# Prompt attention in rounds of four units: scores and weighings of four in a row, the turns in pairs around them, outputs copied by four

## The chip, the cores and the metric

The kernel runs on one core of a Trainium2 chip. The metric is the device time of one execution in microseconds, the median of several runs. All times below are microseconds unless marked ns. Engines: PE is TensorE, DVE is VectorE, ACT is ScalarE, POOL is GpSimd, SP is the engine whose queue issues most transfers.

## What is computed

One layer of a decoder trunk over 2048 prompt tokens and 32 sample tokens: a joint input projection, attention and a convolution module side by side, an output projection, and an MLP. The change touches only the prompt attention. There are 8 heads of 64 and three patterns (window, dilation); the queries of a head are cut into 16 blocks of 128, and each block sees its own 128 keys and, except at the start of a residue class, the 128 before them.

```python
DILATED_PATTERNS = ((128, 1), (512, 4), (2048, 16))
...
logits = jnp.einsum('brnqhd,brnkhd->brnhqk', qb, kc, ...) * (HEAD_DIM ** -0.5) + bias
logits = jnp.where(valid[None, None, :, None], logits, -jnp.inf)
m = jnp.max(logits, axis=-1)
e = jnp.exp(logits - m[..., None])
l = jnp.sum(e, axis=-1)
acc = jnp.einsum('brnhqk,brnkhd->brnqhd', e, vc.astype(jnp.float32))
```

m, l and acc of the three patterns are merged in a later stage.

## The kernel before

The kernel is written with one instruction stream for each engine and semaphores between them; nothing reorders the streams. Its stages run one after the other, with a barrier of all engines between them. The prompt attention is the stage whose tiles are named `pa_`.

Its work is a list of 192 units `(hp, p, t)`: head pair `hp` (4), pattern `p` (0, 1, 2), block of queries `t` (16), in this order. A unit does both heads of its pair. Whether it has a previous block of keys is `has_prev`: in pattern 0 all units but the first, in pattern 1 three of four (not `t` = 0, 4, 8, 12), in pattern 2 none. A unit with one works on 256 keys a head, a unit without on 128. A unit u goes through:

- scores(u), PE: 2 matmuls (one a head, on 64 rows of the array each) into `s_ps`. The trace shows each of these float32 matmuls as two records. Two units share a bank per head, and there are two such banks per head, so unit u waits until unit u-3 has left.
- lower(u), DVE: 2 instructions add the bias, take the extreme and write `score`, four units deep.
- exponential(u), ACT: 2 instructions, in place in `score`.
- turn(u), PE: one transpose for each head and block of keys, 4 (or 2) of 128x128, into `t_ps`, which is two units deep.
- copy_turned(u), DVE: one copy from `t_ps` into `probT`, which is three units deep: it waits for `o_pe`, the count of units weighed, to reach u-2, that is until unit u-3 has been weighed.
- weigh(u), PE: 4 (or 2) matmuls of the values with `probT` into `oT_ps`, on 64 columns of the array each; here too each is two records.
- the result goes from `oT_ps` to `oT` by a copy on ACT, is transposed back by PE (back) into `o_ps`, and copied by DVE into `o_sb`, from where it is stored.

PE, DVE and ACT each run a loop over steps of two units. PE's step s holds the scores of units 2s and 2s+1, the turns of 2s-2 and 2s-1, the back of step s-4 and the weighings of 2s-4 and 2s-3. `oT_ps`, `oT` and `o_ps` hold two units. ACT does in each step the copy of `oT_ps`, four exponentials and, for four of every eight units where the target half is of pattern 1 or 2, a query piece (`query_piece`: a 128x256 copy into `query_run`, from which the scores of the unit eight places later read; 16 pieces a head pair). POOL regroups keys (`key_runs`) and works off part of the convolution.

Of the kernel before, what the change touches and what calls it, by code (L numbers as in the profile page):

```python
# [15 lines left out]
P = 128  # L16
# [78 lines left out]
def build(nc, I, O):  # L95
# [22 lines left out]
    with whole:  # L118
# [104 lines left out]
        with conv:  # L223
# [1172 lines left out]
            with ExitStack() as st:  # L1396
# [30 lines left out]
                oT = sb("oT", [P, 2, 2, P])  # L1427
# [6 lines left out]
                oT_ps, o_ps = ps("oT_ps", [P, 2, P]), ps("o_ps", [P, 2, P])  # L1434
# [13 lines left out]
                STEPS = N // 2  # L1448
# [60 lines left out]
                with nc.Block() as block:  # L1509
                    @block.sync  # L1510
                    def _(sp):
# [29 lines left out]
                        for q in range(3 * PAIRS):  # L1541
                            hp, p = divmod(q, 3)
                            for half in range(2):
# [12 lines left out]
                                sp.wait_ge(o_done, (q * NT + (half + 1) * NT // 2) // 2)  # L1556
# [48 lines left out]
                    def _(pe):  # L1605
# [25 lines left out]
                        def weigh(u):  # L1631
# [5 lines left out]
                            if u >= 2 and u % 2 == 0:  # L1637
                                pe.wait_ge(oT_done, u // 2)
                            for j in range(1 + prev):
                                for hh in range(2):  # L1640
                                    part = slice(hh * DH, hh * DH + DH)
                                    mm = pe.matmul(oT_ps[part, u % 2], vp[hp % 2][:, p, t - prev + j, part],
# [3 lines left out]
                        def back(s):  # L1646
                            pe.wait_ge(oT_done, s + 1)
                            if s >= 1:
                                pe.wait_ge(o_done, s)
                            for i in range(2):  # L1650
                                mm = pe.transpose(o_ps[:, i], oT[:, s % 2, i], ident[:])
                            mm.then_inc(back_pe, 1)

                        for s in range(STEPS + 4):
                            if s < STEPS:
                                scores(2 * s)
                                scores(2 * s + 1)
                            if 1 <= s < STEPS + 1:
                                turn(2 * s - 2)
                                turn(2 * s - 1)  # L1660
                            if s >= 4:
                                back(s - 4)
                            if 2 <= s < STEPS + 2:
                                weigh(2 * s - 4)
                                weigh(2 * s - 3)

                    @block.vector
                    def _(v):
# [25 lines left out]
                        def out_pair(s):  # L1694

                            ch, i = divmod(s, NT // 4)
                            v.wait_ge(back_pe, s + 1)
                            if i == 0 and ch >= 2:
                                v.wait_ge(o_out[ch % 2], out_count(ch - 2))
                            v.tensor_copy(o_sb[:, ch % 2, 2 * i:2 * i + 2], o_ps[:]).then_inc(o_done, 1)  # L1700
# [1602 lines left out]
```

## Time and profile before

| | us |
|---|---|
| median of 3 runs (2705.34 to 2710.91) | 2708.74 |
| profiled execution, own time | 2703.57 |
| its span, first to last instruction | 2701.8 |
| prompt attention, first scores to last output copy | about 614.0 to 886.4 |
| in that stage, one head pair | about 67 |

Read it so: the durations below come from the one profiled execution, whose own time stands 5.17 under the median. The stage is a tenth of the span and has a barrier at its end, so what it takes longer or shorter moves everything behind it.

### The profile page before, as it was taken

To read this page: it belongs to the slowest core of one execution; us is meant where nothing else is said; L and a number is where in the kernel's file an instruction comes from. 1 tells how busy PE (TensorE), PEld (TensorE's weight loads), DVE (VectorE), ACT (ScalarE), POOL (GpSimd) and SP (SyncE) were. 2 spreads that over 40 slices of the span, in tenths; PEclk is the share of its full clock that TensorE was granted. 3 is DMA by queue.
4 is the path that set the end of the run, shared out by engine and by line. 5 is a ranking of instruction groups with operands and counts; after the bars stand their busy time and mean duration, and the time that the engine had idled before them with its cause. 6 is when DMAs were issued, how large, how long until landed. Compare 5 with 4: busy or idle time off the path is not lost.

```text
span 2701.8 us, 45845 instructions
## 1 busy us (share of the span) xinstructions
PE 2571.1 (95%) x16346; PEld 2278.4 (84%) x16346; DVE 1719.2 (64%) x3932; ACT 1220.1 (45%) x3062; POOL 1124.2 (42%) x771
## 2 busy tenths in 40 slices
PE   6999989989999879997999999999999999999998
PEld 3788857877777537875899999999999999999998
DVE  4268889987999447874655555555555555555555
ACT  4343423558888324654344333434443343343332
POOL 0000000008997015663555454545554453555543
PEclk9999989999999989998999999999999999999999
DMA  7767526833444964662424442442353335235222
GB/s 289 279 215 245 182 105 209 278 119 115 140 140 156 379 248 143 223 204 90 137 85 149 164 139 94 137 160 94 126 186 120 112 115 178 94 131 182 79 63 82
DMA packets 314671, 431.24 MB, mean 160 GB/s; under 512 B 23546, under 2 KB 243430, under 8 KB 307910
## 3 DMA queue, kind: packets, MB, share of 16 engines
q1 hardware_dynamic: 292570, 378.88, 41.9%
q0 software_dynamic: 4272, 39.19, 4.1%
q10 hardware_dynamic: 17604, 10.24, 1.2%
q8 instruction: 133, 2.18, 0.3%
q14 instruction: 92, 0.75, 0.1%
HBM read 353.72 MB, written 146.65 MB: 185 GB/s over the span
## 4 chain that ended last, share of the span: by engine, by line
PE 44%; issue 2%; DVE 2%; DMA 2%; POOL 1%; ACT 1%; SPq 1%; DVEq 0%; POOLq 0%; ACTq 0%
PE ff_u_ps L3184 15%; PE ff_u_ps L3186 14%; PE ff_u_ps L3185 14%; DMA gluT<-h_d 1%; POOL ff_w_lo L2829 1%; DMA out_y_prompt_dram<-ff_x_own 0%; DVE ff_wT L3041 0%; SPq L2747 0%; ACT ff_h_hi L2886 0%; POOL ff_h_lo L2838 0%; DMA ff_x_own<-x_d 0%; ACT ff_w_hi L2877 0%; PE ff_out_ps L3179 0%; DVE ff_x_own L3066 0%; DVE ff_wT L3004 0%
## 5 line engine op out<-in xcount | busy, mean ns | idle before, releaser
L2829 POOL TENSOR_TENSOR ff_w_lo<-gluT,ff_w_hi 128x512 fp32r<-128x512 f32 x342 | 458.9, 1349 | 409.2 <-ACT ff_w_hi L2877 409.0
L3184 PE MATMUL ff_u_ps<-ff_a_hi,ff_w_hi 128*128 128x352 f32 (+1 forms) x1536 | 493.3, 321 | 10.7 <-POOL ff_a_lo L2844 9.0
L3185 PE MATMUL ff_u_ps<-ff_a_lo,ff_w_hi 128*128 128x352 f32 (+1 forms) x1536 | 492.7, 321 | 0.0
L3186 PE MATMUL ff_u_ps<-ff_a_hi,ff_w_lo 128*128 128x352 f32 (+1 forms) x1536 | 492.6, 321 | 0.0
L3184 PE MATMUL ff_u_ps<-ff_h_hi,ff_w_hi 128*128 128x352 f32 (+1 forms) x1368 | 441.4, 323 | 16.3 <-DVE ff_h_lo L2989 8.1
L3186 PE MATMUL ff_u_ps<-ff_h_hi,ff_w_lo 128*128 128x352 f32 (+1 forms) x1368 | 438.4, 320 | 0.0
L3185 PE MATMUL ff_u_ps<-ff_h_lo,ff_w_hi 128*128 128x352 f32 (+1 forms) x1368 | 437.3, 320 | 0.0
L3084 DVE SCALAR_TENSOR_TENSOR ff_y<-ff_u_ps,modT,ff_y 128x352 f32<-128x352 f32 (+2 forms) x336 | 188.2, 570 | 316.4 <-PE ff_u_ps L3186 316.2
L2829 POOL TENSOR_TENSOR ff_w_lo<-ff_wT,ff_w_hi 128x512 fp32r<-128x512 f32 x168 | 225.5, 1344 | 272.1 <-ACT ff_w_hi L2877 204.4
L2877 ACT ACTIVATE ff_w_hi<-gluT 128x512 fp32r<-128x512 f32 x342 | 211.5, 626 | 275.6 <-PE ff_u_ps L3186 255.9
L3184 PEld LDWEIGHTS ff_u_ps<-ff_a_hi,ff_w_hi 128*128 128x128 f32 x1536 | 289.8, 189 | 13.2 <-POOL ff_a_lo L2844 10.1
L3185 PEld LDWEIGHTS ff_u_ps<-ff_a_lo,ff_w_hi 128*128 128x128 f32 x1536 | 289.7, 189 | 0.0
L3186 PEld LDWEIGHTS ff_u_ps<-ff_a_hi,ff_w_lo 128*128 128x128 f32 x1536 | 289.5, 188 | 0.0
L3184 PEld LDWEIGHTS ff_u_ps<-ff_h_hi,ff_w_hi 128*128 128x128 f32 x1368 | 258.0, 189 | 23.7 <-issue 11.9
L3185 PEld LDWEIGHTS ff_u_ps<-ff_h_lo,ff_w_hi 128*128 128x128 f32 x1368 | 258.1, 189 | 0.0
L3186 PEld LDWEIGHTS ff_u_ps<-ff_h_hi,ff_w_lo 128*128 128x128 f32 x1368 | 256.9, 188 | 0.0
L2877 ACT ACTIVATE ff_w_hi<-ff_wT 128x512 fp32r<-128x512 f32 x168 | 105.6, 632 | 320.2 <-PE ff_u_ps L3186 234.7
L1738 ACT ACTIVATE pa_score<-pa_score,pa_stat 128x256 f32<-128x256 f32 (+1 forms) x384 | 172.4, 451 | 27.9 <-DVE pa_stat L1683 25.6
L296 DVE SCALAR_TENSOR_TENSOR vu_dwp<-gluT,tapT,vu_dwp 128x512 f32<-128x512 f32 x240 | 161.0, 746 | 0.8 <-DVE rstd L207 0.8
L994 PE MATMUL vu_z_ps<-vu_w_hi,last_hi 128*128 128x512 f32 (+1 forms) x384 | 152.5, 397 | 2.6 <-DVEq L932 2.5
L995 PE MATMUL vu_z_ps<-vu_w_lo,last_hi 128*128 128x512 f32 (+1 forms) x384 | 150.8, 393 | 0.0
L996 PE MATMUL vu_z_ps<-vu_w_hi,last_lo 128*128 128x512 f32 (+1 forms) x384 | 150.6, 392 | 0.0
(354 smaller groups left out, 5004.5 us busy)
## 6 DMA issues: line engine op xcount, KB each, us to landing
gluT<-in_w_ff_dram SPq DMA_DIRECT2D x192, 512.0 KB, 4.9
out_new_k_sample_dram<-in_cache_k_dram SPq DMA_DIRECT2D x40, 511.0 KB, 6.1
out_new_v_sample_dram<-in_cache_v_dram SPq DMA_DIRECT2D x40, 511.0 KB, 6.3
dwq<-in_w_ada_dram SPq DMA_DIRECT2D x32, 512.0 KB, 8.8
gluT<-in_cache_k_dram SPq DMA_DIRECT2D x16, 1024.0 KB, 9.5
gluT<-h_d SPq DMA_DIRECT2D x80, 176.0 KB, 4.7
mx_acc<-acc_d SPq DMA_DIRECT2D x16, 768.0 KB, 8.1
out_new_k_sample_dram<-in_cache_k_dram POOLq DMA_DIRECT2D x3, 4088.0 KB, 17.4
```

The costliest lines, as they stand in the source:

```text
L296: return v.scalar_tensor_tensor(out=out, in0=x, scalar=tap(j, c), in1=out, op0=ALU.mult, op1=ALU.add)
L994: pe.matmul(z, hi, w_hi[:, k, cols], start=k == 0, stop=False)
L995: pe.matmul(z, hi, w_lo[:, k, cols], start=False, stop=False)
L996: mm = pe.matmul(z, lo, w_hi[:, k, cols], start=False, stop=k == KT - 1)
L1738: act.activation(prob[:, u % 4, hh, cols], score[:, u % 4, hh, cols], ACT.Exp, bias=stat[:, p, t, 0, h:h + 1], scale=-1.0, accum_out=stat[ ...
L2829: pool.tensor_tensor(slot_view(w_lo, s), src, slot_view(w_hi, s).bitcast(F32), ALU.subtract).then_inc(w_lod, 1)
L2877: act.activation(slot_view(w_hi, s), src, ACT.Copy).then_inc(w_hid, 1)
L3084: ins = v.scalar_tensor_tensor(out=dst, in0=src[:, 0:gated], scalar=g2, in1=dst, op0=ALU.mult, op1=ALU.add)
L3184: pe.matmul(out, w_hi[:, s % WR, w], hi, start=first, stop=False, skip_group_check=more)
L3185: pe.matmul(out, w_hi[:, s % WR, w], lo, start=False, stop=False, skip_group_check=more)
L3186: return pe.matmul(out, w_lo[:, s % WR, w], hi, start=False, stop=last, skip_group_check=more)
```

## The change

PE, DVE and ACT now loop over rounds of four units. PE's round r holds the scores of units 4r to 4r+3, the turns of 4r-2 and 4r-1, the back of group r-2 (four units), the weighings of 4r-4 to 4r-1, and the turns of 4r and 4r+1. DVE copies 4r-4 and 4r-3, lowers 4r and 4r+1, copies 4r-2 and 4r-1, copies the output of group r-2, and lowers 4r+2 and 4r+3. ACT does the exponentials of 4r and 4r+1, the copy of `oT_ps` for group r-1, the exponentials of 4r+2 and 4r+3, and then up to four query pieces. `oT_ps`, `oT` and `o_ps` hold four units (a copy moves 128x512 where it moved 128x256), `oT` has one buffer where it had two. The depths of `score`, `t_ps`, `probT` and `s_ps` stay.

```diff
-                oT = sb("oT", [P, 2, 2, P])
+                oT = sb("oT", [P, 4, P])
...
-                oT_ps, o_ps = ps("oT_ps", [P, 2, P]), ps("o_ps", [P, 2, P])
+                oT_ps, o_ps = ps("oT_ps", [P, 4, P]), ps("o_ps", [P, 4, P])
...
-                                sp.wait_ge(o_done, (q * NT + (half + 1) * NT // 2) // 2)
+                                sp.wait_ge(o_done, (q * NT + (half + 1) * NT // 2) // 4)
...
-                            if u >= 2 and u % 2 == 0:
-                                pe.wait_ge(oT_done, u // 2)
+                            if u >= 4 and u % 4 == 0:
+                                pe.wait_ge(oT_done, u // 4)
...
-                        for s in range(STEPS + 4):
-                            if s < STEPS:
-                                scores(2 * s)
-                                scores(2 * s + 1)
-                            if 1 <= s < STEPS + 1:
-                                turn(2 * s - 2)
-                                turn(2 * s - 1)
-                            if s >= 4:
-                                back(s - 4)
-                            if 2 <= s < STEPS + 2:
-                                weigh(2 * s - 4)
-                                weigh(2 * s - 3)
+                        for r in range(ROUNDS + 2):
+                            if r < ROUNDS:
+                                for u in range(4 * r, 4 * r + 4):
+                                    scores(u)
+                            if 1 <= r <= ROUNDS:
+                                turn(4 * r - 2)
+                                turn(4 * r - 1)
+                            if r >= 2:
+                                back(r - 2)
+                            if 1 <= r <= ROUNDS:
+                                for u in range(4 * r - 4, 4 * r):
+                                    weigh(u)
+                            if r < ROUNDS:
+                                turn(4 * r)
+                                turn(4 * r + 1)
...
+                        for r in range(ROUNDS + 2):
+                            if 1 <= r <= ROUNDS:
+                                copy_turned(4 * r - 4)
+                                copy_turned(4 * r - 3)
+                            if r < ROUNDS:
+                                lower(4 * r)
+                                lower(4 * r + 1)
+                            if 1 <= r <= ROUNDS:
+                                copy_turned(4 * r - 2)
+                                copy_turned(4 * r - 1)
+                            if r >= 2:
+                                out_four(r - 2)
+                            if r < ROUNDS:
+                                lower(4 * r + 2)
+                                lower(4 * r + 3)
...
-                        for s in range(STEPS + 3):
-                            if s >= 3:
-                                act.wait_ge(o_pe, 2 * (s - 2))
-                                if s >= 5:
-                                    act.wait_ge(back_pe, s - 4)
-                                act.activation(oT[:, (s - 3) % 2], oT_ps[:], ACT.Copy).then_inc(oT_done, 1)
-                            for u in (2 * s, 2 * s + 1):
+                        for r in range(ROUNDS + 1):
+                            for u in (4 * r, 4 * r + 1):
                                 if u < N:
                                     exponential(u)
-                            for u in (2 * s, 2 * s + 1):
+                            if r >= 1:
+                                act.wait_ge(o_pe, 4 * r)
+                                if r >= 2:
+                                    act.wait_ge(back_pe, r - 1)
+                                act.activation(oT[:], oT_ps[:], ACT.Copy).then_inc(oT_done, 1)
+                            for u in (4 * r + 2, 4 * r + 3):
+                                if u < N:
+                                    exponential(u)
+                            for u in range(4 * r, 4 * r + 4):
                                 if u + NT // 2 < N:
                                     query_piece(u)
```

PE in pattern 0 of the second head pair, before: one step of two units, from one back to the next (`pa_o_ps` is the back, `pa_oT_ps` the weighings, `pa_s_ps` the scores, `pa_t_ps` the turns).

```order
L1651 MATMUL pa_o_ps<-ident,pa_oT 128x128 x2
L1642 MATMUL pa_oT_ps<-pa_probT,pa_vp 64x128 x8
L1618 MATMUL pa_s_ps<-pa_kT,pa_qT 128x256 x4
L1628 MATMUL pa_t_ps<-ident,pa_score 128x128 x8
L1651 MATMUL pa_o_ps<-ident,pa_oT 128x128 x2
```

The same place of the changed kernel, one round of four units:

```order
L1618 MATMUL pa_s_ps<-pa_kT,pa_qT 128x256 x8
L1628 MATMUL pa_t_ps<-ident,pa_score 128x128 x8
L1651 MATMUL pa_o_ps<-ident,pa_oT 128x128 x4
L1642 MATMUL pa_oT_ps<-pa_probT,pa_vp 64x128 x16
L1628 MATMUL pa_t_ps<-ident,pa_score 128x128 x8
```

The runs of scores, weighings and backs are twice as long, and the turns of four units are split around the backs and weighings.

ACT at the start of pattern 2 of the second head pair, before (`pa_oT` is the copy of the weighed result, `pa_score` the exponentials, `pa_query_run` the query pieces):

```order
L1738 ACTIVATE pa_score,pa_stat<-pa_score,pa_stat 128x128 x4
L1729 ACTIVATE pa_query_run<-pa_qT 128x256 x2
L1746 ACTIVATE pa_oT<-pa_oT_ps 128x256
L1738 ACTIVATE pa_score,pa_stat<-pa_score,pa_stat 128x128 x4
L1729 ACTIVATE pa_query_run<-pa_qT 128x256 x2
L1746 ACTIVATE pa_oT<-pa_oT_ps 128x256
```

And in the changed kernel (its line numbers are 8 to 11 higher):

```order
L1757 ACTIVATE pa_oT<-pa_oT_ps 128x512
L1746 ACTIVATE pa_score,pa_stat<-pa_score,pa_stat 128x128 x4
L1737 ACTIVATE pa_query_run<-pa_qT 128x256 x4
L1746 ACTIVATE pa_score,pa_stat<-pa_score,pa_stat 128x128 x4
L1757 ACTIVATE pa_oT<-pa_oT_ps 128x512
```

Four query pieces now stand in a row, and the copy of `oT_ps` stands between the exponentials of a round's first and last two units.

## Rows read from the trace of the kernel before

**Rows 1.** Windows, second head pair; columns: stretch, us, busy us, clock.

```profile
680.00:747.00 67.00, 66.66 (x694) 51.59 (x692) 60.88 (x267) 60.00 (x235) 65.11 (x27) 1.00 0.48 139
```

**Rows 2.** Waits, whole stage: us in total, times, longest.

```profile
PE pa_oT_ps L1642 <- ACT pa_oT L1746: 1.3, 4, 0.3
```

**Rows 3.** Timeline, PE, pattern 0: start us, duration us, what.

```profile
764.55 1.09 PE L1642 MATMUL pa_oT_ps<-pa_probT,first_v 128*64 128x128 f32 x16
765.58 1.13 PE L1618 MATMUL pa_s_ps<-first_k,first_q 64*128 64x256 f32 x8
766.64 1.09 PE L1628 MATMUL pa_t_ps<-ident,pa_score 128*128 128x128 f32 x8
767.57 0.38 PE L1651 MATMUL pa_o_ps<-ident,pa_oT 128*128 128x128 f32 x2
```

**Rows 4.** Timeline, PE, pattern 1, two turn-backs four units apart.

```profile
722.32 0.38 PE L1651 MATMUL pa_o_ps<-ident,pa_oT 128*128 128x128 f32 x2
...
728.33 0.38 PE L1651 MATMUL pa_o_ps<-ident,pa_oT 128*128 128x128 f32 x2
```

**Rows 5.** Timeline, PE, one step in pattern 2.

```profile
738.00 0.66 PE L1628 MATMUL pa_t_ps<-ident,pa_score 128*128 128x128 f32 x4
738.49 0.38 PE L1651 MATMUL pa_o_ps<-ident,pa_oT 128*128 128x128 f32 x2
738.80 0.66 PE L1642 MATMUL pa_oT_ps<-pa_probT,pa_vp 128*64 128x128 f32 x8
739.39 0.71 PE L1618 MATMUL pa_s_ps<-pa_key_run,pa_query_run 64*128 64x128 f32 x8
740.04 0.66 PE L1628 MATMUL pa_t_ps<-ident,pa_score 128*128 128x128 f32 x4
```

**Rows 6.** Timeline, ACT, pattern 2.

```profile
738.83 0.39 ACT L1738 ACTIVATE pa_score<-pa_score,pa_stat 128x128 f32<-128x128 f32 x1
739.12 0.19 ACT L1738 ACTIVATION_READ_ACCUMULATOR pa_score<-pa_score,pa_stat 128x1 f32 x1
739.22 0.39 ACT L1738 ACTIVATE pa_score<-pa_score,pa_stat 128x128 f32<-128x128 f32 x1
```

**Rows 7.** Timeline, ACT, pattern 0, two exponentials of 256.

```profile
771.05 0.49 ACT L1738 ACTIVATE pa_score<-pa_score,pa_stat 128x256 f32<-128x256 f32 x1
...
771.54 0.50 ACT L1738 ACTIVATE pa_score<-pa_score,pa_stat 128x256 f32<-128x256 f32 x1
```

**Rows 8.** Timeline, DVE, pattern 0: a copy of turned blocks.

```profile
771.46 0.69 DVE L1692 COPY pa_probT<-pa_t_ps 128x512 f32<-128x512 f32 x1
```

**Rows 9.** Timeline, ACT, two query pieces and what follows.

```profile
762.53 1.22 ACT L1729 ACTIVATE pa_query_run<-first_q 128x256 f32<-128x256 f32 x2
...
763.66 0.36 ACT L1746 ACTIVATE pa_oT<-pa_oT_ps 128x256 f32<-128x256 f32 x1
```

**Rows 10.** Timeline, end of the stage: who follows whom.

```profile
880.88 0.42 DVE L1692 COPY pa_probT<-pa_t_ps 128x256 f32<-128x256 f32 x1
...
881.42 0.20 PEld L1628 LDWEIGHTS pa_t_ps<-ident,pa_score 128*128 128x128 f32 x2 [0.27 <-ACT pa_score L1738]
...
881.83 0.19 ACT L1738 ACTIVATION_READ_ACCUMULATOR pa_score<-pa_score,pa_stat 128x1 f32 x1
...
882.08 0.20 PEld L1628 LDWEIGHTS pa_t_ps<-ident,pa_score 128*128 128x128 f32 x2 [0.46 <-ACT pa_score L1738]
...
882.67 0.66 PE L1642 MATMUL pa_oT_ps<-pa_probT,pa_vp 128*64 128x128 f32 x8
...
883.37 0.38 ACT L1746 ACTIVATE pa_oT<-pa_oT_ps 128x256 f32<-128x256 f32 x1 [1.09 <-PE pa_oT_ps L1642]
...
883.90 0.66 PE L1642 MATMUL pa_oT_ps<-pa_probT,pa_vp 128*64 128x128 f32 x8
...
884.49 0.44 PE L1651 MATMUL pa_o_ps<-ident,pa_oT 128*128 128x128 f32 x2
```

**Rows 11.** Groups by shape, ACT, later stage: a 128x512 copy out of PSUM.

```profile
L2040 ACT ACTIVATE sa_kTt<-sa_k_ps 128x512 f32<-128x512 f32 x31 | 18.5, 597 | 50.4 <-PE sa_k_ps L1902 50.4
```

More of the change, by code:

```diff
@@ L1446, in build @@
                 N = len(units)
-                STEPS = N // 2
+                ROUNDS = N // 4
                 def s_ps(u, hh):
@@ L1641, in weigh @@
                                     part = slice(hh * DH, hh * DH + DH)
-                                    mm = pe.matmul(oT_ps[part, u % 2], vp[hp % 2][:, p, t - prev + j, part],
+                                    mm = pe.matmul(oT_ps[part, u % 4], vp[hp % 2][:, p, t - prev + j, part],
                                                    probT[:, u % 3, hh, j * NB:(j + 1) * NB], start=j == 0, stop=j == prev)
                             mm.then_inc(o_pe, 1)
[L1646 to L1651, printed above, removed]
-                            mm.then_inc(back_pe, 1)
@@ L1654, in _, with back @@
-                        for s in range(STEPS + 4):
-                            if s < STEPS:
-                                scores(2 * s)
-                                scores(2 * s + 1)
-                            if 1 <= s < STEPS + 1:
-                                turn(2 * s - 2)
-                                turn(2 * s - 1)
-                            if s >= 4:
-                                back(s - 4)
-                            if 2 <= s < STEPS + 2:
-                                weigh(2 * s - 4)
-                                weigh(2 * s - 3)
+                        def back(g):
+                            pe.wait_ge(oT_done, g + 1)
+                            if g >= 1:
+                                pe.wait_ge(o_done, g)
+                            for i in range(4):
+                                mm = pe.transpose(o_ps[:, i], oT[:, i], ident[:])
+                            mm.then_inc(back_pe, 1)
```

18 lines of the change are left out of this document (4 added, 14 removed).

## The prediction

> **What bounds the kernel now.** I first asked for the busy time of each engine in a stretch of the prompt attention that covers one head pair. PE is busy for 66.66 of 67.00, DVE for 60.88, ACT for 60.00, and the clock is at its full 2.4 GHz level, 1.00 [rows 1]. So PE sets the pace, with DVE and ACT a tenth behind: a plan that makes them wait on each other more tightly can make either the bound. Next the waits of the stage: the only wait of a weighing on another engine that adds up is for ACT's copy of oT, 1.3 in all, four times, about 0.33 for each head pair [rows 2]. That is where ACT runs late behind its query pieces. Then the timelines, to see how PE's time is made.
>
> In pattern 0 one step (two units) takes 3.33: weighings to scores 1.03, scores to turns 1.06, turns to back 0.93 [rows 3], back to weighings 0.31 [rows 5]. Four units of pattern 1 (one without a previous block) take 728.33 - 722.32 = 6.01 [rows 4]. In pattern 2 a step takes 740.04 - 738.00 = 2.04: turns 0.49, back 0.31, weighings 0.59, scores 0.65 [rows 5].
>
> These pieces hold a part that grows with the number of matmuls and a part that a change of kind costs. Weighings: 16 records take 1.03, 8 take 0.59, so a unit with a previous block takes 0.44, one without 0.22, and 0.15 is left. Turns: 8 take 0.93, 4 take 0.49, so 0.11 each with 0.05 at their start. Back: 2 x 0.11 and 0.09 left. Scores: a row of 8 records lasts 1.13, its starts are spread evenly and the turns begin 0.07 before its end; I take 0.86 of work and 0.20 of change (anything from 0.15, the weighings' price, would do; with 0.15 a round is 0.05 longer). One step so pays 0.20 + 0.09 + 0.15 = 0.44 for changes.
>
> The page TensorEngine Tiling of the Trainium skill, section Tiling Modes, says that changing the tiling mode drains the engine; scores, weighings and turns are of three modes. The trace agrees with 0.09 to 0.20 a change. The page gives no figure, and turns followed by scores, which the new order has once a round, are in no row here.
>
> **The change, part by part.** *PE's order.* Four units pay two steps' changes now, 0.88. A round pays scores to turns 0.20, back to weighings 0.09, weighings to turns (as weighings to back in the tail: 884.49 - 883.90 = 0.59 for 8 records, so 0.15 again [rows 10]) and turns to scores. The last is unknown: bounds 0 (no change at all, as turns to back) and 0.20 (the dearest row); I take 0.09, that of back to weighings, since there too a full-array transpose comes before. Sum 0.53, so 0.35 less. A round by PE alone:
>
> - pattern 0: 1.72 + 0.20 + 0.93 + 0.53 + 1.76 + 0.15 + 0.93 + 0.09 = 6.31 (now 6.66);
> - pattern 1: one unit of four is smaller in scores (1.06 - 0.65 over two units, 0.20), weighings and turns (0.22 each): 5.67 (now 6.01);
> - pattern 2: 0.90 + 0.20 + 0.49 + 0.53 + 0.88 + 0.15 + 0.49 + 0.09 = 3.73 (now 4.08).
>
> *Four weighings in a row against a probT of three.* copy_turned(4r-1) may start only when unit 4r-4 has been weighed, and weigh(4r-1) needs that copy. The weighing of one unit with a previous block is a row of 8 records, 0.66 long, and what waits for it starts 0.04 later (883.37 against 882.67 + 0.66) [rows 10]. The copy lasts 0.69 [rows 8] and PE follows a copy by 0.12 (881.42 against 880.88 + 0.42) [rows 10]. So from the first weighing to the fourth: 0.66 + 0.04 + 0.69 + 0.12 = 1.51, where PE comes there after 3 x 0.44 = 1.32: 0.20 lost. Pattern 1, whose first unit is the small one: 0.44 + 0.04 + 0.69 + 0.12 = 1.29 against 1.10, 0.20. Pattern 2: 0.44 + 0.04 + 0.42 (the copy in [rows 10]) + 0.12 = 1.02 against 0.66, 0.36. In the order now the weighings of two units have copies made a step ahead, and no such wait stands in the trace. Rounds are then 6.51, 5.87 and 4.09: -0.15, -0.14, +0.01. Bounds of this loss: 0, if DVE or PE take the signal up faster than the rows show, and 0.28, with 0.20 for the take-up (881.42 stands behind other possible causes).
>
> *The oT copy between the exponentials.* ACT's copy for group r-1 waits for the last weighing of the round, and behind it on ACT stand the exponentials of 4r+2 and 4r+3, for which the turns of the next round wait, behind which stand that round's back and weighings. That is a closed ring. Pattern 2, from the first weighing: fourth weighing starts 1.02, ends 0.44 later, 0.04 to ACT: 1.50. The copy is 128x512: such copies out of PSUM last 0.597 on ACT [rows 11]; the copy of 256 lasts 0.36 [rows 9], and on ACT the next instruction starts some 0.09 before the one ahead has ended (739.22 against 739.12 + 0.19 [rows 6]), so I take 0.50 until the next starts (bounds 0.36, no dearer than today's, and 0.60). Four exponentials at 0.39 (739.22 - 738.83 [rows 6]): 3.56, the last reading ends 0.09 later, PE takes it up 0.06 later (882.08 against 881.83 + 0.19 [rows 10]): 3.71. Then one unit's turn 0.25 and the back 0.53: 4.49 until the next first weighing. PE alone needs 4.09. So a round of pattern 2 takes 4.49, +0.41 against 4.08. In pattern 0 the exponentials are 0.49 apart [rows 7]: weighings 1.52 + 0.66, 0.04 + 0.50 + 1.96 + 0.15, turn 0.47 and back 0.53 make 5.83, under 6.51; pattern 1 likewise 5.6 under 5.87. Hidden there.
>
> *Four query pieces in a row.* They come in 4 rounds of a head pair: one in pattern 0, two in 1, one in 2. A piece takes (763.66 - 762.53) / 2 = 0.57 [rows 9]. Behind them stand the exponentials of 4r+4 and 4r+5, wanted by the turns after the next weighings. From the end of the last weighing to the second of those turns, ACT: 0.04 + 0.50 + two units + 4 x 0.57 + two units + 0.15. PE: what the round holds in between.
>
> - pattern 0: ACT 6.89, PE 6.91: nothing.
> - pattern 1: ACT 6.69; PE -0.07 + 0.71 + 0.09 + 1.72 + 0.93 + 0.53 + 1.91 + 0.25 = 6.07: 0.62 lost, twice.
> - pattern 2: ACT 0.04 + 0.50 + 1.56 + 2.28 + 1.56 + 0.15 = 6.09; PE, held by the ring to 2.25 for its second turn, then 0.25 + 0.53 + 1.39 + 0.25 = 4.67: 1.42 lost.
>
> Now a step has at most two pieces and PE turns a unit a whole step after its exponentials were due, so only the 0.33 in [rows 2] shows; that goes.
>
> *Outputs by four.* Half as many copies on DVE, which is busy nine tenths of a round now [rows 1] and gets no more to do; none lies on PE's path. Nothing. The section Optimizing Scalar/DVE Operations of the Trainium skill's page Perfetto Trace Analysis has both sides: grouping small operations saves a fixed cost each (about 125 ns on DVE out of PSUM, which gives an estimate of 48 x 0.125 = 6 of DVE's time), but where an engine that is not saturated makes others wait, breaking instructions up lets work finish sooner. By the first the change gains, by the second it loses; the ring above is the second case. SP's waits for stores, the loads behind them and POOL's key runs follow the same units at most two units later, with a head pair of 67 to hide in. Start and end: the drain after the last scores holds two full rings of four instead of steps of two, about +1; the first weighings come with fewer changes, about -1: 0.
>
> **Sum.** A head pair: pattern 0 4 x -0.15 = -0.60; pattern 1 4 x -0.14 + 2 x 0.62 = +0.68; pattern 2 4 x 0.41 + 1.42 = +3.06; together +3.1. Four pairs +12.6, less the 1.3 = +11. The profiled execution's own time, 2703.57 (span 2701.8), would become 2714.6. The median of the runs shown is 5.17 above that execution; against it the forecast is 2708.74 + 11, some 2720.
>
> **Rivals.**
> *Fewer changes win.* If the four weighings find their copies and the ring closes below PE's own round, only the first edit is left: 48 x 0.35 = 17 and the 1.3: 2690. For it speaks that these 0.35 are the surest part; against it that three buffers in probT force the wait whatever the order on DVE. It decides from a copy taken up within 0.6 of the first weighing in pattern 0. A half-way case: the weighings' waits stand, but ACT keeps up everywhere (copy at 0.36, pieces spread by slack): 4 x (-0.60 - 0.56 + 0.04) - 1.3 = -6: 2703.
> *A tie.* The ring at the low bounds (4.35) and half the piece losses: 4 x (-1.16 + 1.08 + 1.33) - 1.3 = +4, and turns to scores free (-0.09 in the 32 rounds that PE sets, -3): +1: 2710.
> *Dearer.* Turns to scores at 0.20, the copy wait at 0.28, the ring at its high end (4.6): +0.19 in 32 rounds and +0.11 in 16: +19: 2728.
>
> **Chances.** The forecast's mechanism with a size from +4 to +17: 0.55. Dearer than that: 0.09. Tie: 0.15. Half-way gain 0.13, full gain 0.08. The likeliest gives 2720. A range of 2701 to 2733 leaves out the full gain and the far end of the dearer case. A difference of about 0.2%, 5.4, is what a measurement of this kernel can tell from none. Slower by more than that: most of the forecast (0.49) and the dearer case, 0.58. Within: the rest of the forecast, the tie, a little of the half-way case: 0.22. Faster: 0.20. The likeliest case's own range is 2713 to 2726.
>
> **What would show it.** In the profile after: rounds of about 6.5, 5.9 and 4.5 between backs; a wait of about 0.2 to 0.4 of the weighings for probT's copy, some 48 times; in pattern 2 turns that wait for the exponentials each round, and ACT without idle time there; one gap of about 1.4 on PE at the start of each pattern 2 and about 0.6 twice in pattern 1. DVE's idle time grows. Rounds of 6.3 in pattern 0 would refute the probT wait, rounds of 3.8 in pattern 2 the ring. The forecast is wrong if the end of one weighing row is earlier for DVE than the row's modelled end, or if turns to scores costs far more than any change seen.

## The result and the profile after

| | us |
|---|---|
| median of before, 8 runs (2705.34 to 2711.93) | 2710.72 |
| median of after, 8 runs (2715.65 to 2726.48) | 2720.53 |
| ratio after to before | 1.0038 [1.0027, 1.0049] |
| profiled execution of after, own time | 2715.65 |
| its span | 2713.8 |
| prompt attention, first scores to end of last output copy | 613.92 to 896.9 = 283.0 (before: 614.0 to 886.4 = 272.4) |

The kernel is slower by 9.8, a little under 0.4%. The stage is 10.6 longer, so the loss is made there. Below, a stage length is always first scores to end of last output copy, in one profiled execution. The stage starts between 613.9 and 621.5 in the profiled executions of this study, though nothing ahead of it was changed, so stage lengths compare more sharply than spans or times. TensorE's clock is no cause of the loss: in both kernels it is at 0.50 (the 1.2 GHz level) for the first 5.3 (before) and 4.9 (after) of the stage, and at 1.00 in all the rest of it.

Busy time of the same 67 us as in [rows 1], after:

```profile
680.00:747.00 67.00, 64.17 (x668) 50.19 (x668) 57.17 (x238) 56.35 (x212) 65.11 (x27) 1.00 0.48 139
```

PE, DVE and ACT are all less busy than in [rows 1], at the same clock, and fewer matmuls fit in (668 records against 694). So nobody works more: they wait on each other. The waits of the whole stage, after (us in total, times, longest), say who (PEld is PE's weight loads):

```profile
ACT pa_oT L1757 <- PE pa_oT_ps L1642: 43.5, 32, 2.4
DVE pa_probT L1695 <- PE pa_oT_ps L1642: 35.3, 48, 1.2
...
PEld pa_t_ps L1628 <- ACT pa_score L1746: 28.1, 66, 1.1
PEld pa_oT_ps L1642 <- DVE pa_probT L1695: 16.3, 63, 0.4
...
PE pa_t_ps L1628 <- ACT pa_score L1746: 9.4, 25, 0.9
...
PE pa_oT_ps L1642 <- DVE pa_probT L1695: 2.5, 16, 0.2
```

None of the lines on `pa_oT_ps` was among the large waits before; there the weighings had one, for ACT's copy [rows 2], and it is gone. The turns waited for ACT before as well, but less:

```profile
PEld pa_t_ps L1628 <- ACT pa_score L1738: 12.0, 35, 0.7
```

48 is the number of rounds: in each of them DVE waits for a weighing and the weighings then wait for DVE. In pattern 0 DVE's side of it is

```profile
704.79 0.69 DVE L1695 COPY pa_probT<-pa_t_ps 128x512 f32<-128x512 f32 x1 [0.69 <-PE pa_oT_ps L1642]
```

and PE's timeline, after, over one round of pattern 0, from back to back:

```profile
696.96 0.60 PE L1651 MATMUL pa_o_ps<-ident,pa_oT 128*128 128x128 f32 x4
697.49 2.18 PE L1642 MATMUL pa_oT_ps<-pa_probT,pa_vp 128*64 128x128 f32 x32
699.60 1.09 PE L1628 MATMUL pa_t_ps<-ident,pa_score 128*128 128x128 f32 x8
700.62 2.00 PE L1618 MATMUL pa_s_ps<-pa_kT,pa_qT 64*128 64x256 f32 x16
702.55 1.09 PE L1628 MATMUL pa_t_ps<-ident,pa_score 128*128 128x128 f32 x8
703.48 0.60 PE L1651 MATMUL pa_o_ps<-ident,pa_oT 128*128 128x128 f32 x4
```

The round takes 703.48 - 696.96 = 6.52. Turns to scores take 700.62 - 699.60 = 1.02, 0.09 more than 8 turns (0.93): the changeover that no row of before showed costs 0.09. Weighings to turns take 2.11, where 16 blocks at 0.11 and a changeover of 0.15 are 1.91: the 0.20 is the wait inside the row of weighings.

The same engine, after, in pattern 2: a round that stands beside query pieces, then one without.

```profile
739.45 0.60 PE L1651 MATMUL pa_o_ps<-ident,pa_oT 128*128 128x128 f32 x4
739.98 0.88 PE L1642 MATMUL pa_oT_ps<-pa_probT,pa_vp 128*64 128x128 f32 x12
741.02 0.44 PE L1642 MATMUL pa_oT_ps<-pa_probT,pa_vp 128*64 128x128 f32 x4 [0.16 <-DVE pa_probT L1695]
742.08 0.44 PE L1628 MATMUL pa_t_ps<-ident,pa_score 128*128 128x128 f32 x2 [0.62 <-ACT pa_score L1746]
742.85 0.44 PE L1628 MATMUL pa_t_ps<-ident,pa_score 128*128 128x128 f32 x2 [0.33 <-ACT pa_score L1746]
...
745.14 0.60 PE L1651 MATMUL pa_o_ps<-ident,pa_oT 128*128 128x128 f32 x4
...
749.37 0.44 PE L1628 MATMUL pa_t_ps<-ident,pa_score 128*128 128x128 f32 x2 [0.16 <-ACT pa_score L1746]
749.65 0.60 PE L1651 MATMUL pa_o_ps<-ident,pa_oT 128*128 128x128 f32 x4
```

The fourth weighing starts 741.02 - 739.98 = 1.04 after the first, behind DVE's copy; the turns wait for ACT 0.62 and 0.33, behind four query pieces. This round takes 745.14 - 739.45 = 5.69, the next 749.65 - 745.14 = 4.51. ACT over the same time:

```profile
739.03 2.22 ACT L1737 ACTIVATE pa_query_run<-pa_qT 128x256 f32<-128x256 f32 x4
...
742.70 0.57 ACT L1757 ACTIVATE pa_oT<-pa_oT_ps 128x512 f32<-128x512 f32 x1
...
747.19 0.60 ACT L1757 ACTIVATE pa_oT<-pa_oT_ps 128x512 f32<-128x512 f32 x1 [0.84 <-PE pa_oT_ps L1642]
747.68 0.39 ACT L1746 ACTIVATE pa_score<-pa_score,pa_stat 128x128 f32<-128x128 f32 x1
```

The pieces hold ACT for 2.22. In the round without pieces ACT is idle for 0.84 ahead of its copy, and the next exponential starts 0.49 after the copy.

| round, back to back | forecast | after |
|---|---|---|
| pattern 0 | 6.51 | 6.52 |
| pattern 1 | 5.87 | 5.87 |
| pattern 1 beside query pieces | 6.49, twice | 6.54 and 6.14 (the second already holds scores of pattern 2) |
| pattern 2 | 4.49 | 4.51 |
| pattern 2 beside query pieces | 5.91 | 5.69 |
| a head pair (second, first scores to first scores) | 66.9 + 2.8 | 69.31 (before 66.91) |

### The profile page after: what moved, and what is told of

It is laid out like the page before. It is cut to its first block, busy times and chain, and to the rows that moved or that the text cites. A ratio compares the mean times of both kernels' runs of the same rounds, so it can differ in the third digit from the quotient of the medians.

```text
span 2713.8 us, 45606 instructions
## 1 busy us (share of the span) xinstructions
PE 2571.4 (95%) x16346; PEld 2279.9 (84%) x16346; DVE 1715.0 (63%) x3884; ACT 1214.2 (45%) x3014; POOL 1123.0 (41%) x771
## 3 DMA queue, kind: packets, MB, share of 16 engines
q8 instruction: 132, 2.16, 0.3%
## 4 chain that ended last, share of the span: by engine, by line
PE 44%; issue 2%; DVE 2%; DMA 2%; POOL 1%; ACT 1%; SPq 1%; DVEq 0%; POOLq 0%; ACTq 0%
PE ff_u_ps L3195 15%; PE ff_u_ps L3197 14%; PE ff_u_ps L3196 14%; DMA gluT<-h_d 1%; POOL ff_w_lo L2840 1%; DMA out_y_prompt_dram<-ff_x_own 0%; DVE ff_wT L3052 0%; ACT ff_h_hi L2897 0%; SPq L2758 0%; POOL ff_h_lo L2849 0%; DMA ff_x_own<-x_d 0%; SPq L257 0%; ACT ff_w_hi L2888 0%; PE ff_out_ps L3190 0%; DVE ff_x_own L3077 0%
```

## The experiments

Two theories stand against each other. **The forecast's:** PE's order saves its 0.35 a round, and three things give it back and more: the fourth weighing's wait for the third buffer of `probT`, the ring through ACT's copy of `oT_ps`, and the query pieces in a row. **Rival:** the longer rows themselves are dearer, or a later stage was disturbed, and no buffer or piece would bring the time back. Each run is compared with the kernel before as timed beside it (its medians: 2707.48 for probT4, few_pieces, few_pieces_before and late_oT; 2706.68 for spread, probT4_spread and probT4_few; 2706.95 for the three runs with keys; 2707.40 and 2705.69 for the last two). The medians bear the stage lengths out roughly: over the kernel before, after is at +9.8, and by that measure probT4 gains 5.4, few_pieces 5.1, spread 7.6, each uncertain by some 4.

**probT4.** A fourth transposed buffer, laid into tiles that are free by then.

```diff
+                def probT_of(u):
+                    if u % 4 < 3:
+                        return probT[:, u % 4]
+                    return first_b if u >= NT else spare
...
-                            if u >= 3:
-                                v.wait_ge(o_pe, u - 2)
+                            if u >= 4:
+                                v.wait_ge(o_pe, u - 3)
```

> The changed kernel with a fourth buffer behind probT, so that copy_turned(u) waits for unit u-4 instead of u-3; nothing else moves. Theory of the prediction (fourth weighing waits for its copy, and this wait is also a link of the ring in pattern 2): rounds of 6.3 in pattern 0, 5.67 in pattern 1, about 4.15 in pattern 2, and no gap between the third and fourth weighing; 12 us less than the changed kernel, so about 2 less than the kernel before. Rival (ACT's total work is what holds the rounds, the probT wait only fills time that would be lost anyway): pattern 0 gains, patterns 1 and 2 don't; 3 us less than the changed kernel, still 6 or 7 more than before.

Measured: 2711.88 against 2707.48, ratio 1.0013 [1.0002, 1.0025]; stage 274.8, so 8.2 shorter than after. A round of pattern 2 in its timeline:

```profile
749.66 0.60 PE L1657 MATMUL pa_o_ps<-ident,pa_oT 128*128 128x128 f32 x4
750.19 0.88 PE L1648 MATMUL pa_oT_ps<-pa_probT,pa_vp 128*64 128x128 f32 x12
750.90 0.39 PE L1648 MATMUL pa_oT_ps<-first_b,pa_vp 128*64 128x128 f32 x4
...
753.79 0.60 PE L1657 MATMUL pa_o_ps<-ident,pa_oT 128*128 128x128 f32 x4
```

The fourth weighing (now from `first_b`) starts 0.71 after the first instead of 1.04, and the round takes 4.13, down from 4.51. Pattern 0 falls to 6.32, pattern 1 to 5.66: PE's own rounds of the forecast (6.31 and 5.67). So the wait is real and of the forecast's size. The stage gained 8.2 and not 12 because the rounds beside query pieces did not move (pattern 1: 720.82 to 727.36, still 6.54): there ACT is last, and an earlier weighing only waits longer for it.

**few_pieces and few_pieces_before.** Query pieces for the first two runs of a total of sixteen only, in the kernel after and in the one before; for the other fourteen the scores read what an earlier run left, so part of the computation is left out. One more line lets the scores wait for no more pieces than those.

```diff
-                            if p == 0 or k >= 4:
+                            if p == 0 or k >= 4 or run_of(hp, p, half) > 1:
```

> The changed kernel without the query pieces of all runs after the first two; the scores there read what an earlier run left, so this part of the computation is left out. Theory (four pieces in a row hold up the turns behind them): the losses of 0.6 twice and 1.2 once for each head pair vanish, 2.4 to 2.6 a pair, about 9 us less than the changed kernel and about the time of the kernel before; rounds without pieces stay at 6.5, 5.9 and 4.5. Rival (rounds are long because of the ring and the probT wait alone, pieces lie in ACT's idle time): under 3 us less.

> The kernel before without the same query pieces (the same part of the computation left out). Theory (in steps of two the pieces are nearly hidden): 1.3 us less than before, within what can be told. Rival (pieces cost as much in the old order, so that the new order's piece rounds are nothing new): 5 to 10 less.

Measured: after without them 2712.22, ratio 1.002 [1.0011, 1.0029], stage 274.3 (8.7 shorter); before without them 2704.65, ratio 0.9987 [0.9979, 0.9996], stage 270.2 (2.2 shorter). The rounds inside pattern 2 of the kernel after, 5.69 and 4.51, are then both 4.51, and the two beside pieces in pattern 1 fall from 6.54 and 6.14 to 5.87 and 5.64. The same pieces cost 2.2 in steps of two and 8.7 in rounds of four.

**late_oT.** ACT copies `oT_ps` behind the exponentials of 4r+2 and 4r+3 instead of ahead of them.

```diff
+                            for u in (4 * r + 2, 4 * r + 3):
+                                if u < N:
+                                    exponential(u)
                             if r >= 1:
                                 act.wait_ge(o_pe, 4 * r)
...
-                            for u in (4 * r + 2, 4 * r + 3):
-                                if u < N:
-                                    exponential(u)
```

> The changed kernel with ACT's copy of oT_ps after the exponentials of 4r+2 and 4r+3 instead of ahead of them. Theory (rings through ACT): the ring weighings, oT copy, exponentials, turn is cut, but in pattern 2 another closes: copy of the fourth unit, output copy, lowering of 4r+2 and 4r+3 on DVE, four exponentials, oT copy, back, weighings, by the same rows 1.8 + 1.56 + 0.7 + 0.53 = 4.6, so pattern 2 stays at 4.5 to 4.6; the pieces no longer stand behind the wait for the last weighing plus two units of exponentials, so the losses in pattern 1 go (0.6 twice) and that in pattern 2 shrinks: 5 to 8 us less than the changed kernel. Rival (the place of the oT copy is all that costs in pattern 2): pattern 2 at 4.1, 11 or more less.

Measured: 2724.57, ratio 1.0059 [1.0046, 1.0071], stage 287.0: 4.0 longer than after. The expectation missed in sign. But the 4.0 is not all the edit's order. The second head pair takes 69.61 from back to back where it took 69.32, 0.3 longer, some 1.2 in four. The rest, some 2.7, stands in two places, in the third and the fourth head pair, where TensorE's granted clock fell to 0.50 for about 3.4 each: the two rounds there take 11.77 and 11.49, the same two of the second head pair 10.29. In the kernel after it did so nowhere behind the stage's start. The first place, PE and then the windows view (columns as in [rows 1]):

```profile
820.06 0.44 PE L1628 MATMUL pa_t_ps<-ident,pa_score 128*128 128x128 f32 x2 [0.85 <-ACT pa_score L1746]
...
821.20 1.94 PE L1618 MATMUL pa_s_ps<-pa_key_run,pa_query_run 64*128 64x128 f32 x16
...
822.00:824.50 2.50, 2.50 (x19) 2.28 (x16) 1.36 (x9) 2.34 (x11) 2.44 (x2) 0.50 0.87 235
```

The same sixteen score records take 1.16 at 751.59, at full clock, though the turns ahead of them had waited for the same 0.85 and 0.33. In the 3 ahead of the fall PE was busy for 1.66. Why the clock fell in two head pairs and not in the second is not shown. ACT in a round of pattern 2 at full clock:

```profile
754.53 0.21 ACT L1746 ACTIVATION_READ_ACCUMULATOR pa_score<-pa_score,pa_stat 128x1 f32 x1
755.66 0.40 ACT L1746 ACTIVATE pa_score<-pa_score,pa_stat 128x128 f32<-128x128 f32 x1 [0.93 <-DVE pa_stat L1686]
...
757.22 0.57 ACT L1760 ACTIVATE pa_oT<-pa_oT_ps 128x512 f32<-128x512 f32 x1
```

The exponentials of 4r+2 wait for DVE's lowering. On DVE that lowering stands behind copy_turned(4r-1), and that waits for the weighing of 4r-4. So both what ACT could do first and what it could do second hang on PE's weighings, and in the kernel after, the copy fills a gap in which ACT has nothing else. Behind the exponentials it comes later and holds up the back: the round takes 4.58 where it took 4.51. Whether that reading holds is tried further down, in all_late_oT.

**spread.** The query pieces of a round are not four in a row: three ahead of the copy of `oT_ps` (those of units 4r-1, 4r, 4r+1), one at the round's end (4r+2). Nothing is left out.

```diff
+                            for u in (4 * r - 1, 4 * r, 4 * r + 1):
+                                if 0 <= u and u + NT // 2 < N:
+                                    query_piece(u)
                             if r >= 1:
                                 act.wait_ge(o_pe, 4 * r)
...
-                            for u in range(4 * r, 4 * r + 4):
+                            for u in (4 * r + 2,):
```

> The changed kernel with the four query pieces of a round spread over three places on ACT: two after the exponentials of 4r+1 (ahead of the oT copy, where ACT waits about 1.5 us for the last weighing anyway), one at the round's end, one in the next round ahead of the oT copy; the same copies, none left out. Theory (the pieces cost what stands in a row behind the wait): no wait of turns for exponentials in pattern 1, about 0.2 a head pair left in pattern 2, the stage 8 us shorter than that of the changed kernel (283.0 from the first scores to the last output copy), some 275. Rival (ACT's total work counts, wherever the pieces stand): under 3 shorter.

Measured: 2708.93 against 2706.68, ratio 1.0009 [1.0000, 1.0017], stage 274.2 (8.8 shorter than after). It recovers all that leaving the pieces out did, but for 0.13 in the round of pattern 2 beside them (4.64 against 4.51). What costs is their place, hardly their work.

**probT4_spread and probT4_few.** Both edits together; and the fourth buffer without the pieces.

> The changed kernel with the fourth probT buffer and the pieces spread. Theory: the fourth buffer gave 8.2 of the 12.2 because in the rounds with pieces ACT was late anyway; with the pieces out of the way it gives all, rounds of 6.3, 5.67 and 4.15: the stage near 263 to 265, 8 to 9 under the kernel before (272.4), and the time 7 to 9 us under the kernel before. Rival (the fourth buffer had a cost of its own or only parts of its gain can be had): stage 267 or more, a time within 5 of before.

> The fourth buffer, and the query pieces of all but the first two runs left out (that part of the computation is not done). It is the floor for the round order with ACT relieved: by theory rounds of 6.3, 5.67 and 4.15 everywhere, 16 x (6.3 + 5.67 + 4.15) less the small units' parts, a stage of about 262, against 270.2 for the old order without the same pieces. Rival: something else in the rounds costs, and the stage stays over 266.

Measured: 2704.65, ratio 0.9992 [0.9982, 1.0001], stage 271.8; and 2705.16, ratio 0.9999 [0.9988, 1.0010], stage 270.9. Both stages missed by 7 to 9, though the second head pair's rounds are as short as expected (6.31, 5.66 and 4.13; in probT4_spread one of pattern 2 keeps 4.64, beside pieces). The rows that tell why are in the third and the last head pair, PE of probT4_few:

```profile
802.62 1.16 PE L1624 MATMUL pa_s_ps<-pa_key_run,pa_query_run 64*128 64x128 f32 x16 [1.41 <-POOL pa_key_run L1583]
862.55 2.08 PE L1624 MATMUL pa_s_ps<-pa_key_run,pa_query_run 64*128 64x128 f32 x16 [5.85 <-POOL pa_key_run L1583]
```

and POOL of the same kernel just before:

```profile
855.17 2.85 POOL L1587 TENSOR_SCALAR pa_tap_x<-gluT,tapT 128x1024 f32<-128x1024 f32 x1
858.10 2.34 POOL L1588 TENSOR_TENSOR dwq<-dwq,pa_tap_x 128x1024 f32<-128x1024 f32 x1
860.61 3.71 POOL L1583 COPY pa_key_run<-pa_kT 128x1024 f32<-128x1024 f32 x2 [0.17 <-POOL dwq L1588]
```

POOL copies the regrouped keys of pattern 2 only after six multiply-and-add pairs of the convolution, seven in the last head pair, some 5.4 each, in one queue. POOL is busy 65.10 of 67 in this kernel too, as in [rows 1]; with head pairs of 67 or 69 no scores waited for its copies, with head pairs of 64 they do.

**probT4_spread_keys, probT4_few_keys, keys_before.** The key runs of pattern 2 go ahead of some of those pairs.

```diff
-                            late_pairs(4)
-                            late_pairs(2 if hp + 1 < PAIRS else 3)
-                            if hp + 1 == PAIRS:
-                                pool.sem_inc(dw_done, 1)
+                            late_pairs(6 if hp + 1 < PAIRS else 5)
                             key_runs(hp, 2, 0)
-                            if hp + 1 < PAIRS:
-                                late_pairs(2)
+                            late_pairs(1 if hp + 1 < PAIRS else 2)
+                            if hp + 1 == PAIRS:
+                                pool.sem_inc(dw_done, 1)
                             key_runs(hp, 2, 1)
                             if hp + 1 < PAIRS:
-                                late_pairs(3)
+                                late_pairs(4)
```

> The kernel with a fourth transposed buffer and spread query pieces, all of its work done, with GpSimd's order changed: a head pair's third and fourth key runs (those of pattern 2) are copied one or two multiply-and-add pairs earlier. In probT4_spread TensorE waited for GpSimd's key runs twice, 1.12 us at 802.25 and 5.90 us at 862.24, where the copies stood behind six or seven multiply-and-add pairs of 5.39 us each. Theory (GpSimd's key runs had become the bound, and swallowed what the two edits give together): both waits go, the stage is 7.0 shorter, 271.8 - 7.0 = 264.8 us, and the time is some 2704.7 - 7 = 2698, a ratio to the kernel before of about 0.9965, faster than both kernels. Rival (the gain of the two edits is capped elsewhere, by the DMAs or by the turn of a head pair): the wait moves to another releaser and the stage stays at 270 to 272, ratio 0.999.

> The same order of GpSimd's work in the kernel with a fourth transposed buffer and query pieces for the first two runs alone (the other runs' scores read old query pieces, so those outputs are not attention outputs). In probT4_few TensorE waited for GpSimd's key runs 1.41 us at 802.62 and 5.85 us at 862.55. Theory: both go, stage 270.9 - 7.3 = 263.6 us, time about 2705.2 - 7.3 = 2697.9, ratio about 0.996. Rival: stage stays at 270 to 271. The distance to probT4_spread_keys tells what the query pieces still cost when spread: about 1 us by the theory.

> The kernel before with GpSimd's new order alone. There TensorE waits for no key run anywhere in the stage, so by the theory nothing changes: stage 272.4 to 272.9 us, ratio 1.000 (0.999 to 1.001). If it comes out faster by over 0.2%, GpSimd's order is worth something by itself and the other two runs must be read against this one.

Measured: 2698.30 against 2706.95, ratio 0.9969 [0.9958, 0.9980], stage 262.7; 2697.69, ratio 0.9966 [0.9953, 0.9979], stage 261.9; and 2710.49, ratio 1.0012 [1.0002, 1.0022], stage 272.5. The two waits for POOL are gone, and the first one's stage is 9.1 shorter than in probT4_spread, 2.1 more than the waits themselves (1.12 and 5.90). Those 2.1 go to TensorE's clock: towards the end of the 5.90, in which PE stood idle, the granted clock fell, and it stayed at 0.50 for 6.8, about 1 of that still in the wait and the rest with PE at work. Behind the wait scores to turns take 2.01, turns to back 1.75 and back to weighings 1.00, where they take 1.09, 0.93 and 0.53 at full clock, 2.2 more together. probT4_spread, the scores behind the wait and the windows view:

```profile
862.24 2.08 PE L1624 MATMUL pa_s_ps<-pa_key_run,pa_query_run 64*128 64x128 f32 x16 [5.90 <-POOL pa_key_run L1583]
...
862.00:868.00 6.00, 5.76 (x38) 5.21 (x40) 3.21 (x14) 2.71 (x10) 2.02 (x2) 0.50 0.01 3
```

In probT4_spread_keys the clock stays at 1.00 from 621.5 to the stage's end. In the kernel before the new order does nothing to the stage; that run is 0.12% slower by its median (the interval ends just above none), and in the profiled execution the excess lies ahead of the stage, which starts at 621.07 where it started at 614.00. Nothing was changed there, and no row here explains it. The first of the three leaves nothing out, and is faster than both kernels. The 0.8 between the first two stages is what the spread pieces still cost.

**all_late_oT.** probT4_spread_keys with late_oT's edit.

> probT4_spread_keys (stage 262.7 us) with the edit of late_oT: ACT's copy of oT_ps behind the exponentials of units 4r+2 and 4r+3 instead of ahead of them. With three transposed buffers that edit cost 4.0 us. Theory (it cost there because DVE's lowering of 4r+2 stands behind a copy into probT that waits for a weighing, so the exponentials came late and kept the copy of oT_ps back): with four buffers DVE does not wait for the weighings, the lowerings are early, ACT no longer idles for the last weighing, and pattern 2's round falls from 4.13 towards DVE's own work of some 3.9; 16 rounds of 0.2 are 3, so the stage is 260 to 262, and the time about 2696. Rival (the copy behind the exponentials lengthens the path from the weighings to the back whatever the buffers): the stage is again some 4 longer, 266 to 267, and the time about 2702.

Measured: 2697.32 against 2707.40, ratio 0.9965 [0.9952, 0.9978], stage 262.2. PE in pattern 2 of its second head pair:

```profile
741.26 0.66 PE L1655 MATMUL pa_o_ps<-ident,pa_oT 128*128 128x128 f32 x4
741.84 0.88 PE L1646 MATMUL pa_oT_ps<-pa_probT,pa_vp 128*64 128x128 f32 x12
...
745.07 0.66 PE L1655 MATMUL pa_o_ps<-ident,pa_oT 128*128 128x128 f32 x4
```

A round of 3.81, where it was 4.13 with the copy first. The edit that cost 4.0 with three buffers pays with four (a head pair takes 63.07, from back to back in pattern 0: 704.03 to 767.10; with the copy first it took 64.26). So the reading of late_oT's miss holds in its sense; it explains the 0.3 a head pair there, not the clock's share. By the medians this run cannot be told from probT4_spread_keys. The stage is only 0.5 shorter, since in the last head pair the scores wait for POOL again:

```profile
868.55 1.79 PE L1622 MATMUL pa_s_ps<-pa_key_run,pa_query_run 64*128 64x128 f32 x16 [2.99 <-POOL pa_key_run L1583]
```

POOL's copy that it waits for starts at 866.61, behind two pairs. The clock falls to 0.50 here too, for 3.4, and the round takes 7.99 against 4.50 in the second head pair.

**all_late_keys.** all_late_oT with POOL's last key run one pair earlier.

```diff
-                            late_pairs(1 if hp + 1 < PAIRS else 2)
-                            if hp + 1 == PAIRS:
-                                pool.sem_inc(dw_done, 1)
+                            late_pairs(1)
                             key_runs(hp, 2, 1)
-                            if hp + 1 < PAIRS:
-                                late_pairs(4)
+                            late_pairs(4 if hp + 1 < PAIRS else 1)
+                            if hp + 1 == PAIRS:
+                                pool.sem_inc(dw_done, 1)
```

> all_late_oT (stage 262.2 us) with GpSimd's last key run one multiply-and-add pair (5.4 us) earlier, ahead of the last pair instead of behind it. In all_late_oT TensorE waited 2.99 us for that run at 868.55 and the round around it took 7.99 where its neighbours take 4.4 and 3.8. Theory (that copy's place in GpSimd's queue is all that stands between the last head pair and the others): the wait goes, the round is 3.8 to 4.4, the stage 258 to 259 us, the time about 2697.3 - 3.7 = 2693.6, ratio about 0.995. Rival (the wait moves elsewhere, or the end of the convolution, now 2 us later, holds up the loads of the stage behind): the stage is as short, but the time stays at 2697, ratio 0.9965.

Measured: 2694.16 against 2705.69, ratio 0.9951 [0.9939, 0.9963], stage 621.38 to 879.73 = 258.4. The last head pair's wait for POOL is gone (the round that took 7.99 takes 4.49), and with it the fall of the clock. One wait of scores for POOL is left, 0.66 at 794.57 in the third head pair (0.38 in all_late_oT). The stage is 14 shorter than that of the kernel before, the time 11.5. Part of what the stage gains is handed on: in the stage behind, PE waits longer for a load.

```profile
895.28 3.67 PE L1919 MATMUL sa_k_ps<-ident,gluT 128*128 128x128 f32 x16 [4.66 <-DMA gluT<-in_cache_k_dram]
```

The wait for this load was 1.30 in the kernel before, 1.39 after and 1.67 in all_late_oT. It is the next thing to look at.

## Why the prediction was right

**Fewer changes of kind, -0.35 a round.** Right. With the waits taken away one by one, pattern 0 and 1 take 6.32 and 5.66 and pattern 2 takes 3.81, against the forecast's 6.31, 5.67 and 3.73 for PE alone. In patterns 0 and 1 that is 0.34 and 0.35 less than before; in pattern 2 it is 0.27, and what holds the last 0.08 was not tried. The changeover that had to be chosen between 0 and 0.20 was taken as 0.09 and is 0.09. On the drain at a change of tiling mode (the Trainium skill, TensorEngine Tiling, section Tiling Modes) the traces agree: a change between the three shapes costs 0.09 to 0.20, and turns to back, which share a shape, cost none.

**The fourth weighing's wait.** Right in place and size: 1.04 from first to fourth weighing in pattern 2, forecast 1.02; the rounds are 6.52 and 5.87, forecast 6.51 and 5.87; a fourth buffer removes just this. That the 1.04 came out so close is partly luck: the copy began 0.08 later than forecast and PE followed it 0.06 sooner (last section).

**The ring in pattern 2.** Right in size, 4.51 against 4.49. One sign was described wrongly: ACT was to be without idle time there, but it idles 0.84 a round, because the ring runs through PE's weighings and ACT waits for them. The step from that to late_oT's expectation was the error: a gap on an engine is of use only if the work to be put in it is ready, and it was held by the same weighings by way of DVE.

**Four query pieces in a row.** Right in mechanism, somewhat too large. Forecast 0.62 + 0.62 + 1.42 = 2.66 a head pair. Against the same rounds of few_pieces those beside pieces are 6.54 - 5.87 = 0.67, 6.14 - 5.64 = 0.50 and 5.69 - 4.51 = 1.18 longer, 2.35. few_pieces keeps the first two runs, and so the 0.67 of the first head pair: 3 x 2.35 + 1.68 = 8.7, just its gain. The second 0.62 and the 1.42 were too large, for the better part because of the pieces' own price: four of them were taken as 2.28, and ACT's next exponential starts 2.28, 2.16 and 2.13 after their start in the three places.

**The wait that goes, 1.3, and outputs by four.** The weighings' wait for ACT's copy is gone. DVE's output copies fall from 24 of 414 ns to 12 of 680 ns a head pair, 9.9 to 8.2, which is 0.15 for each copy saved; some 7 of DVE's time in the stage, and none of it on the path. The Trainium skill, Perfetto Trace Analysis, section Optimizing Scalar/DVE Operations, has about 0.125 for each as the engine's busy time, and about twice that as profiled latency; the 0.15 of these rows is near the first. The same section says that, where an engine that is not saturated makes others wait, breaking its instructions up may let work finish sooner. ACT's copy in the ring is such a case (idle 0.84 ahead of it, the turns behind it late), but no run here splits the copy, so what that would give is not shown.

**Sum.** Forecast +11, measured +9.8 by the medians and +10.6 in the stage. Per head pair +2.4 against 2.8, so 9.6 of the 10.6; the last 1 lies at start and end, where 0 was forecast. The 2.4 is made of three terms that the runs without pieces separate (second head pair: before 66.91, without pieces 66.37; after 69.32, without pieces 66.95): the rounds themselves +0.58, forecast +0.48; the pieces in rounds of four +2.37, forecast +2.66; and the pieces in steps of two, which go, -0.54, forecast -0.33. So the closeness of the sum is in part luck: a head pair was forecast 0.4 too long, 1.6 in four, and start and end 1 too short.

**What the experiments' own expectations missed.** Gains do not add while two causes cover each other: probT4's 12 were only 8.2 because of the pieces, and buffer and spread together are worth 20.3 (283.0 to 262.7), but only once POOL's queue no longer holds back 9.1 of it. The prediction looked at POOL and found it with "a head pair of 67 to hide in"; that holds at 67 and not at 64. And no expectation reckoned with TensorE's clock, which made some 2.7 of late_oT's 4.0 and 2.1 of the 9.1.

## What to carry to other kernels

When runs of one kind are made longer, compare their length with the depth of every buffer between the engines: a row of four against three buffers makes a wait inside the row, and the fix is one buffer, not the old order. Small jobs that an in-order engine does between urgent ones (query pieces here) must be spread when the rounds grow. When the bound has been moved, read the busy time of the engines that "have slack" against the new, shorter period, and look in the last round of the stage, where their debt is due. And before a difference of a few microseconds is put down to an order of instructions, read the granted clock over that stretch.

## What was not expected of the hardware

A change between the scores' and the turns' shape of matmul costs differently by direction: turns to scores 0.09, scores to turns some 0.20. The forecast had chosen the second; after, it can be read, since there are rows of two lengths: from the first of 16 score records to the turns 702.55 - 700.62 = 1.93, from the first of 8 it was 1.06 [rows 3], so 8 records take 0.87 and 0.19 is left (in pattern 2 744.30 - 743.21 = 1.09 and 0.65 [rows 5] leave 0.21). PE takes DVE's copy into `probT` up faster than the tail's rows said [rows 10]: in pattern 2 the fourth weighing starts 0.48 after the copy's start, 741.02 against 740.54, with the copy 0.42 long, so 0.06 after its end and not the 0.12 that the forecast took.

```profile
740.54 0.42 DVE L1695 COPY pa_probT<-pa_t_ps 128x256 f32<-128x256 f32 x1 [1.02 <-PE pa_oT_ps L1642]
```

The sum still came out since the copy began later than forecast: 740.54 is 0.56 after the first weighing, where 0.48 was taken.

TensorE's granted clock can fall to 0.50 in the middle of a busy stage without a long pause: in late_oT it did so twice, at 821 and 893, where PE's longest single waits were 0.85 and 0.83 and PE was busy for 1.66 and 1.84 of the 3 before. In the second head pair of the same execution the same waits brought no fall.
